# Hybrid attention and Mamba-2 layer: from three stages in a row to two token halves in one program, with the mixer units in four pieces between the dense products

## The reference, cut to what matters

```python
proj = h @ w_in        # 1024 -> q,k,v,z_a,z_m,xbc,dt,g_a,g_b  (77 tiles of 128 columns)
y_a = sliding_window_attention(q, k, v, ...)          # 16 heads, window 128
y_a = (y_a * jax.nn.silu(z_a)) @ w_attn_proj
xbc = jax.nn.silu(causal_depthwise_conv(xbc, conv_w, conv_b))
y = ssd_chunked(xs, dt, a, bm, cm)                    # 32 heads, chunks of 128, carried state
y = rms_norm((y + d_skip * xs) * jax.nn.silu(z_m))    # per group of 512
y_b = y @ w_ssm_proj
merged = sigmoid(g_a) * y_a + sigmoid(g_b) * y_b
return x + gate * (merged @ w_out)
```

## Time and profile before

| | us |
|---|---|
| median of 3 runs | 3410.92 (3410.88 to 3412.6) |
| profiled execution, its span | 3408.3 (its own time is not listed apart; the span is 2.6 under the median of the runs) |
| PE busy | 3048.3 |
| DVE busy | 1495.0 |
| ACT busy | 1182.8 |
| POOL busy | 552.5 |

### The profile page before, as it was taken

The page is one execution under the profiler, slowest core; times in us unless marked ns, Lnnn a source line. Parts: engine busy times, 40 slices in busy tenths (PEclk is TensorE's granted clock), DMA queues, the critical chain, the costliest instruction groups (busy, mean ns, idle before and its releaser), DMA issues. The chain is left out here.

```text
span 3408.3 us, 43274 instructions
## 1 busy us (share of the span) xinstructions
PE 3048.3 (89%) x14967; PEld 2427.2 (71%) x14967; DVE 1495.0 (44%) x1803; ACT 1182.8 (35%) x2177; POOL 552.5 (16%) x601
## 2 busy tenths in 40 slices
PE   2399999999999999999999477787877699999999
PEld 2287778888888888888888355555554588888787
DVE  3601111111114444442111699989999345444321
ACT  1514442212223333331111477777777211111121
POOL 0000000000000000000000277676777100000000
PEclk7599999999999999999999688888888899999999
DMA  5211111111111111111121365655565687787543
GB/s 193 93 56 56 70 60 74 74 74 74 74 74 56 74 74 74 74 74 74 74 74 56 117 177 169 175 164 169 169 176 153 207 271 256 251 262 264 196 155 117
DMA packets 287442, 436.39 MB, mean 128 GB/s; under 512 B 22080, under 2 KB 217456, under 8 KB 276464
## 3 DMA queue, kind: packets, MB, share of 16 engines
q1 hardware_dynamic: 263392, 320.02, 30.5%
q10 hardware_dynamic: 14768, 81.97, 5.9%
q0 software_dynamic: 9216, 33.56, 2.5%
HBM read 295.60 MB, written 139.87 MB: 128 GB/s over the span
## 5 line engine op out<-in xcount | busy, mean ns | idle before, releaser
L472 PE MATMUL proj_psum_acc<-h_hi,proj_w_hi 128*128 128x512 f32 x2464 | 663.7, 391 | 13.1 <-DVE proj_w_lo L529 13.1
L472 PE MATMUL proj_psum_acc<-h_lo,proj_w_hi 128*128 128x512 f32 x2464 | 659.4, 389 | 0.0
L472 PE MATMUL proj_psum_acc<-h_hi,proj_w_lo 128*128 128x512 f32 x2464 | 659.1, 389 | 0.0
L472 PEld LDWEIGHTS proj_psum_acc<-h_hi,proj_w_hi 128*128 128x128 f32 x2464 | 463.1, 188 | 113.5 <-DVE proj_w_lo L529 13.5
L472 PEld LDWEIGHTS proj_psum_acc<-h_lo,proj_w_hi 128*128 128x128 f32 x2464 | 463.2, 188 | 96.2
L472 PEld LDWEIGHTS proj_psum_acc<-h_hi,proj_w_lo 128*128 128x128 f32 x2464 | 463.2, 188 | 96.1
L981 POOL TENSOR_TENSOR mix_xend<-mix_xdt,dec_toend 128x512 f32<-128x512 f32 x64 | 66.7, 1041 | 1917.6 <-DVE mix_xdt L1054 1917.6
L1301 PE MATMUL merge_psum_acc<-merge_a_hi,merge_w_hi 128*128 128x512 f32 x1024 | 319.1, 393 | 27.6 <-DVE merge_a_lo L1352 22.1
L1301 PE MATMUL merge_psum_acc<-merge_a_lo,merge_w_hi 128*128 128x512 f32 x1024 | 316.9, 391 | 0.0
L1301 PE MATMUL merge_psum_acc<-merge_a_hi,merge_w_lo 128*128 128x512 f32 x1024 | 316.6, 391 | 0.0
L550 DVE SCALAR_TENSOR_TENSOR proj_res<-proj_u,proj_res 128x2048 f32<-128x2048 f32 x48 | 110.0, 2292 | 434.3 <-ACT proj_u L498 386.7
(11 more groups left out here) (182 smaller groups left out, 3630.5 us busy)
## 6 DMA issues: line engine op xcount, KB each, us to landing
mix_row<-scr_rowcum SPq DMA_DIRECT2D x64, 512.0 KB, 4.1
scr_xbc<-proj_res ACTq DMA_DIRECT2D x24, 1024.0 KB, 3.9
merge_side<-scr_g SPq DMA_DIRECT2D x48, 512.0 KB, 4.7
scr_m<-merge_res POOLq DMA_DIRECT2D x48, 512.0 KB, 8.1
scr_zm<-proj_res ACTq DMA_DIRECT2D x16, 1024.0 KB, 3.9
scr_g<-proj_res ACTq DMA_DIRECT2D x16, 1024.0 KB, 3.9
mix_xt<-scr_xbc SPq DMA_DIRECT2D x64, 256.0 KB, 3.5
mix_zt<-scr_zm SPq DMA_DIRECT2D x64, 256.0 KB, 4.3
```

The costliest lines, as they stand in the source:

```text
L472: last = nc.tensor.matmul(acc[:, b, c * MM:(c + 1) * MM], wv[:, kk, :], hv[:, kk, c * MM:(c + 1) * MM], start=(kk == 0 and step == 0), sto ...
```

## The change: one list that all engines follow

The three stages `project`, `mixers` and `merge` (with `decays`) become one block, `trunk`. The tokens are cut in two halves ("slabs") of 1024. The dense work is first the projection of slab 0, then that of slab 1, then the passes `attn`, `y0`, `y1`, `out` of slab 0, then the same of slab 1. A list `ORDER`, made when the program is built, holds every dense product, every small step, and each mixer unit in four pieces. Each engine's stream walks this list and emits its share of each entry. All loops are unrolled.

- A dense product `("mul", w, c)` is now 512 tokens wide: 24 matmuls into one of two PSUM banks of a ring. `sum`, `turn` and `ysum` take their place in the same ring, and an entry waits until the one two before it was evacuated by ACT. There are 436 products of 24 matmuls, 10464 matmuls, as before (7392 + 3072).
- Mixer units -2 to 29 are spread over the projection of slab 1 up to the first `g` tile, units 30 to 64 over the `g` tiles and the passes `attn`, `y0`, `y1` and half of `out` of slab 0. PE's piece 0 turns the probabilities and makes the scan's outputs, piece 1 weighs the values, piece 2 makes the scores of the unit after next, piece 3 prepares it.
- Weights have one landing buffer `raw` instead of two, and are split two tiles ahead; the load of tile w + 3 waits for the split of tile w + 2.
- The group norm is made in each unit (`ysum`): a matmul with `ones`, then Ln and Exp on ACT and four multiplications on DVE. `merge` loads no norm row and makes no `norm_a`.
- In slab 0 the input of the next pass is loaded at the end of a pass (`load_half`) into the only free buffer and split there (`split`). In slab 1 it is loaded chunk by chunk (`load_chunk`) beside the pass, into a second pair of buffers; the input of `out` comes straight from `res`.
- All loads and stores are issued by SP.
- The masked bias tables are made in `setup` instead of at the start of `mixers`.

Its core, from the new code:

```diff
+    for w, t in enumerate(TILES):
+        lag = {"norm": "sum", "out": "turn"}.get(t.kind)
+        p, j = divmod(w - MERGE0, NJ)
+        for c in range(4 if t.kind == "dt" else 2):
+            seq.append(("mul", w, c))
...
+            if p == 3 and j >= NJ // 2:
+                seq.append(("chunk", p + 1, 2 * (j - NJ // 2) + c))
+            elif 4 <= p < 6 and c == 1:
+                seq.append(("chunk", p + 1, j))
+            elif p == 6 and c == 0 and j >= 1:
+                seq.append(("chunk", p + 1, j - 1))
...
+        if w == MERGE0 - 1 or (0 <= p < 3 and j == NJ - 1):
+            seq += [("split", p + 1, 0), ("split", p + 1, 1)]
...
+        for n in range(n0, n1):
+            for q in range(4):
+                i = i0 + (i1 - i0) * (4 * (n - n0) + q) // (4 * (n1 - n0))
+                if q == 0 and 0 <= n - 1 < UNITS:
+                    mixed.setdefault(i, []).append(("ysum", n - 1, 0))
+                mixed.setdefault(i, []).append(("mix", n, q))
...
+            def ringed(op, w, c):
+                r = RING[op, w, c]
+                bank = ring[:, r % 2, :]
+                if r >= 2:
+                    pe.wait_ge(evacuated, r - 1)
...
+                elif op == "ysum":
+                    if w >= 1:
+                        act.wait_ge(y_normed, w)
+                    nc.scalar.activation(rsb[:, :], bank[:, 0:P], ACT.Ln, bias=k["eps"][:, :], scale=1.0 / (R * HD)).then_inc(evacuated, 1)
+                    act.wait_ge(evacuated, r + 1)
+                    nc.scalar.activation(rsb[:, :], rsb[:, :], ACT.Exp, scale=-0.5).then_inc(rs_made, 1)
...
+                elif op == "chunk":
+                    load_chunk(w, c)
...
+                    if c == (3 if w == 0 else 1):
+                        if w >= 2:
+                            store_upto(w - 1)
+                        if j == NJ - 1 and -1 <= p < 3:
+                            for cc in range(2):
+                                load_half(p + 1, cc)
+                        if w + 3 < NT:
+                            load_w(w + 3)
+                        if MERGE0 <= w + 1 < NT:
+                            load_sides(w + 1)
+                            if TILES[w + 1].kind == "more":
+                                load_prev(w + 1)
```

More of the change, by code:

```diff
@@ L18 @@
 import math
+from collections import namedtuple
 from contextlib import ExitStack
@@ L68, in bucket_onehot @@
     return (b[None, :] == np.arange(BUCKETS)[:, None]).astype(np.float32)
[L71 to L83, removed]
+SLAB = S // 2
+HALF = 512
+PASSES = ["attn", "y0", "y1", "out"]
+PASS_KIND = {"attn": "first", "y0": "more", "y1": "more", "out": "out"}
+NJ = D // P
+G = SG
+XT = R * HD // P
+PAIRS = GRP // 2
@@ new lines, with weight_order @@
+UNITS = NBLK * G
+Tile = namedtuple("Tile", "kind name e slab")
+def weight_order():
+    tiles = [Tile("dt", "dt", 0, 0)]
+    for s in range(2):
+        tiles += [Tile(kind, name, e, s) for kind, _, count, name in KINDS if name != "dt" for e in range(count)]
+    for s in range(2):
+        tiles += [Tile(PASS_KIND[what], what, e, s) for what in PASSES for e in range(NJ)]
+    return tiles
+TILES = weight_order()
+NT = len(TILES)
+SLAB1 = 1 + sum(c for _, _, c, n in KINDS if n != "dt")
+MERGE0 = 2 * SLAB1 - 1
@@ new lines, with __init__, put @@
+ORDER = whole_order()
+RING = {d: i for i, d in enumerate([d for d in ORDER if d[0] in RINGED])}
+BEFORE = {}
+for _kind in ("norm", "silu", "conv", "first", "more", "out"):
+    for _w, _t in enumerate(TILES):
+        if _t.kind == _kind:
+            BEFORE[_w] = 2 * sum(1 for _u in TILES[:_w] if _u.kind == _kind)
+class Place:
+    def __init__(self, nc, start, end):
+        self.nc, self.at, self.end = nc, start, end
+    def put(self, name, shape, d=F32):
+        at = self.at
+        self.at = at + (4 * math.prod(shape[1:]) + 31) // 32 * 32
+        assert self.at <= self.end, (name, self.at - self.end)
+        return self.nc.alloc_sbuf_tensor_at(name, shape, d, offset=at)
@@ new lines, in product @@
+            def product(w, c):
+                t = TILES[w]
+                bank = ring[:, RING["mul", w, c] % 2, :]
+                pe.wait_ge(lo_made, w + 1)
+                if w >= MERGE0:
+                    p = (w - MERGE0) // NJ
+                    pe.wait_ge(a_lo_made, splits(p, c))
+                    hi, lo = a_of(p)
+                else:
+                    hi, lo = h[c // 2 if t.name == "dt" else t.slab]
+                cols = slice(c % 2 * HALF, (c % 2 + 1) * HALF)
+                for kk in range(KT):
+                    for step, (wv, hv) in enumerate(((w_hi[w % 2], hi), (w_hi[w % 2], lo), (w_lo[w % 2], hi))):
+                        last = nc.tensor.matmul(bank, wv[:, kk, :], hv[:, kk, cols],
+                                                start=(kk == 0 and step == 0), stop=(kk == KT - 1 and step == 2))
+                last.then_inc(multiplied, 1)
@@ new lines, in exponential_inputs, with segments @@
+            def exponential_inputs(m):
+                g, s, b, t = unit(m)
+                act.wait_ge(row_loaded[b], 16 * loads(m, 2))
+                if m >= 2:
+                    act.wait_ge(y_made, m - 1)
+                nc.scalar.activation(cx[:, b, :, :], row[:, b, :, :], ACT.Exp).then_inc(row_exp, 1)
+            def segments(m, rs):
+                g, s, b, t = unit(m)
+                act.wait_ge(row_exp, m + 1)
+                for r in rs:
+                    last = nc.scalar.activation(row[:, b, r, :], row[:, b, r, :], ACT.Relu, scale=-1.0,
+                                                bias=dec["cum"][:, t * SH + g * R + r:t * SH + g * R + r + 1])
+                last.then_inc(seg_made, 1)
```

1664 lines of the change are left out of this document (820 added, 844 removed).

## The result

The changed kernel takes **3490.98 us** (median of 4 runs, 3487.67 to 3502.07) against 3410.9 for the kernel before (4 runs, 3409.37 to 3412.6): a ratio of 1.0241, 95% interval 1.0225 to 1.0257. It is slower, where the prediction said faster, and lies 16 us above its range. The profiled execution has a span of 3491.0 us, at a mean granted clock of 0.941.

A forecast was written before the change was run, and what follows sets the result against it. PE was taken to bound projection and merge, DVE the mixers. PE's own work with start and end, 3083 us, plus waits of 264 gave 3347, forecast as 3350; its own range was 3270 to 3420, the 8-in-10 range 3230 to 3475.

The forecast's parts named there:

- item 4: Pass starts of slab 1's merge: the last chunk is issued behind a weight load that waits for a split; 43 us.
- item 5: Slab 1 tile loops waiting for loads and splits (y0 14.8 us per tile), and chunks beside slab 0's out: 42 us.
- item 1: Gaps between products holding pieces 3 and 0, or 0 and 1: PE waits 2.4 or 2.6 us each, 52 together.
- item 2: Projection tiles with sums for q and k: waits of 35 us in slab 1 and 9 in slab 0, 44 together.
- item 3: The four input splits of slab 0: waits of 13, 10, 8 and, before out, 16 us; 47 together.
- the new order "at the same price": Dense products: matmuls ordered 2, then 1 per weights, all into one bank, still cost 5.45 us per product of 24.
- 6 the rest: Remaining waits: turns 6, conv tiles with units 8, SP's late loads in slab 0 10, lower clock 12; 36 us.
- rival B: Merge loads: SP's burst lands 9 us after issue, not 6.5, lengthening tiles and pass starts; 3462 us, chance 0.22.
- Rival C: ACT: a table change costs two loads' time, each Ln and Exp pair 2.6 us longer; 3479 us, chance 0.04.
- rival A: Waits hide as ACT and DVE work ahead; only late loads and a third of the rest count; 3196 us, chance 0.20.
- rival D: Mixer pieces stand between products but nothing overlaps, so units keep their 742 us; 3516 us, chance 0.04.
- The signs named: Trace marks: right, gaps over 10 us before merge passes, y0 tiles about 15 us; wrong, matmuls above 0.23 us at full clock.

The follow-up runs named there:

- Run 12: The changed kernel with only a pad of 224 bytes, so that h0 and a1 start at 153216: 3463.75 us.
- run 1: The kernel before with h_hi and h_lo alone shifted by 32 bytes per partition: 3462.87 us, ratio 1.0150 to the kernel before.
- run 8: The kernel of run 6 with one more pad of 128 bytes, h0 and a1 moved to 153216: 3332.88 us, ratio 0.9773 to the kernel before.
- run 10: The kernel before with the projection's weight tiles moved by 32 bytes and the moving operands left in place: 3460.4 us, ratio 1.0145.
- run 3: The changed kernel with SP issuing the next pass's chunk before weight tile w + 3, sides and prev: 3388.1 us, ratio 0.9933 to the kernel before.
- Run 6: The kernel of run 4 with tiles at multiples of 128 bytes, and weight tile w + 2 split behind the mixer pieces, not ahead: 3352.16 us.
- run 7: The kernel of run 4 with tiles at multiples of 128 bytes, leaving out the inverse root of the scan's norm: 3321.73 us.
- run 11: The kernel of run 8, leaving out the inverse root of the norm of q and k (scaled copies instead): 3305.44 us.
- run 4: The changed kernel with SP issuing chunk, sides and prev before weight tile w + 3: 3378.02 us, ratio 0.9899 to the kernel before.

## Why the prediction was wrong, point by point

The steps that failed, in the prediction's own terms: items 4 and 5, where SP reaches the late loads much later, and they land later, than the sum had it (152 us, not 85); items 1 to 3, the waits in mixer pieces, norm tiles and splits (204 us, not 143); and the new order "at the same price", which left out where the tiles lie (27 us, not 0). The mechanisms of the items were there; their sizes were not.

Forecast and measured, in us. Waits are read from the first and last matmul of each product, less PE's own work in the gap:

| term | forecast | measured |
|---|---|---|
| start | 168.4 | 165.8 |
| a product that is served well | 5.45 | 5.44 |
| a unit's own work on PE | 7.5 | 7.4 |
| place of `h0`, `a1` | none | 27 |
| 1 pieces without a product | 52 | 74 |
| 2 norm tiles | 44 | 70 |
| 3 splits of slab 0 | 47 | 60 |
| 4 pass starts of slab 1 | 43 | 69 |
| 5 loops and chunks | 42 | 83 |
| 6 the rest | 36 | 25 |

The differences from the place down add up to 144, and 3491 less 3347 is 144 too. But the start and the units' own work came out 9 us less (2.6 and 64 x 0.1), so some 9 us of the time stand in no row.

The range was too narrow by its own terms. Units at 7.0 to 8.8 us move the time by -32 and +83, waits by a quarter by 66: together 3252 to 3499, where 3270 to 3420 was given.

- **PE's own work**, at the upper clock, was right. In `za` and `zm` of slab 1 (1341.0 to 1668.6 us) PE is busy for 327.60 of 327.60 us at clock 1.00 with 46 products and 10.5 units: (327.6 - 46 x 5.44) / 10.5 = 7.4 us. The idea of the change works there without any wait.
- **The step "I take the new order at the same price"** was right about the order and wrong about the product: what changed the price was where the tiles lie, which I had not read. Run 12 shows the 27 us by itself, and runs 1, 8 and 10 that it hangs on the distance to the weights; why the distance counts stays open.
- **Items 4 and 5** failed by their size. The mechanism stood there: SP reaches the late loads behind a weight load that waits for a split. But I let the last of the burst land in 6.5 us in the loop and in 5.4 at the starts; it was 9.2. So the loop of `y0` took 17.2 us in four tiles and 16.0 in the mean, not 14.8; the starts of `attn`, `y0`, `y1` and `out` took 12.5, 18.8, 22.1 and 15.7 us, where the forecast had 11.5 before `attn`, 12.8 and 13.5 before the `y` passes and 5 before `out`; and the chunks beside `out` of slab 0 some 25 and not 5. The landing alone does not explain the starts. Before `y1` the split that SP waits for ends at 3259.18 us, 8.7 us after the last matmul of `y0` began, and not 3, since ACT and DVE had first to wait for the chunk before, which landed 8.74 us after its issue; the last chunk then took 9.26. A burst that lands in 9 us is rival B's mechanism (it decided from 8.4 us on), and by it the time was to be 3462. That this is near 3491 is in part luck: B made all 24 tiles of `attn`, `y0` and `y1` in slab 1 longer by 2.5 us, but in `y1` seven of the eight took 11.2 to 12.6 us. Nor did I see that the order could be had otherwise: run 3 took back 103 us by moving one load in SP's list, with the landing still at 8.6 us.
- **Items 1 to 3** were 61 low together. The nine gaps with pieces 3 and 0 cost 4.8 each, not 2.4, since DVE's stream holds a whole merge ahead of the denominators, for which I had taken the best case. Run 6 shows the weight split's part; the merge's part is read from the chain above, not shown by a run. The eight with 0 and 1 cost 3.8, not 2.6: POOL's maskings and the two table changes stand in one chain, run 7.
- **Rival C** (a table change of two loads' time) is refuted by the rows under "Table changes". But a table change of 1.28 us costs PE time where it lies on its path: 56 us for 128 of them and 27 us for 80 in runs 7 and 11. The list has them in the 26 us of the ten gaps and in part of the 44 of the norm tiles.
- **Rivals A and D**: part of A's gain was there to be had (runs 4, 6, 8: 3332.88), but not in this order. D is out: in `za` and `zm` of slab 1 all overlaps.
- **The signs named**: gaps before each pass and `y0` tiles waiting for `a_lo` were there, and so was a mark of being wrong, matmuls of over 0.23 us at full clock. One sign missed: ACT was to be busy for about 300 us more than 1183 and was for 510 more, of which the 211 table loads are 271.

Whether the change wins or loses hangs on one term: with the chunk first alone it is faster than the kernel before by 0.7% (0.5 to 0.8), with the pad alone still slower by 1.6%.

## What to carry to other kernels

When one engine issues all loads in a fixed order, read what each load stands behind: one that waits for a split holds up all that follow. Moving the others ahead was worth 113 us here, more than the 61 us that I had forecast for the whole change; but a load that itself waits for a buffer, as the sides of `out` do, holds up what follows just as well, and cost 24 of them. Take a landing time from rows with the same burst, or take the range. And when a change moves tiles in memory, compare the spacing of the same matmuls before and after before blaming their order.

## What the runs showed of the hardware that I had not expected

The spacing of dense 128x128 by 128x512 fp32r matmuls, each with its own weight load, depends on the distance between moving operand and weights modulo 256 bytes per partition: 0.2267 us at 0, 0.2290 at 64, 0.2324 at 128, 0.2333 at 32 and at 224. Moving either of the two by 32 bytes costs about 50 us in 7392 matmuls: 49 by the spacing, 51 by the times of runs 1 and 10. Why it is so, no run tells; distances other than these five were not tried. And at full clock a product that follows other work of PE starts with up to eight matmuls spaced by more, the first above all (0.34 us, or 0.63 behind piece 0 of a unit): 5.34 to 5.66 us from first to last start, against 5.21 behind another product. In `za` and `zm` of slab 1 that is 0.9 of the 7.4 us of a mixer unit.
